# The first expert query ahead of the last input norm, its squares summed per token

## The reference

```
z = rmsnorm(h, norm2_g)                 # h / sqrt(mean(h*h) + EPS) * norm2_g
q = z @ peer_wq                         # 8 heads, two halves of 128 each
s1, s2 = q_half1 . keys1, q_half2 . keys2        # 128 + 128 scores per head
top 16 of each, their 256 sums, top 16 of these -> expert numbers, gate = softmax
act = gelu(u[expert] . z);  w = gate * act;  out = sum over experts of w * v[expert]
result = rmsnorm(h + out, norm_f_g)
```

## Time and profile before

| | |
|---|---|
| median of 3 runs | 2670.79 us (2670.49 to 2677.07) |
| span of the profiled execution, first to last instruction | 2671.2 us (the only time given for it) |
| busy PE, DVE, ACT, POOL | 2250.8, 2099.3, 1146.8, 639.4 us |
| traffic | 732.02 MB, 274 GB/s over the span |
| chain that ended last | DVE 23%, PE 17%, DMA 13%, issue 3% |

### The profile page before, as it was taken

One profiled execution on the slowest core, in us unless ns is written; L12 is line 12 of the kernel. 1 busy time (PEld: TensorE's weight loads), 2 busy tenths in 40 slices (PEclk: granted clock), 3 DMA queues, 4 the chain that ended last, 5 costly groups with the idle time before them and its releaser, 6 DMA issues.

```text
span 2671.2 us, 32182 instructions
## 1 busy us (share of the span) xinstructions
PE 2250.8 (84%) x11476; PEld 1809.5 (68%) x11476; DVE 2099.3 (79%) x2971; ACT 1146.8 (43%) x1721; POOL 639.4 (24%) x834
## 2 busy tenths in 40 slices
PE   8999989999999999989999964444555558999997
PEld 7997778888888888879888841111222225777776
DVE  6986647665566556578766999989999999999997
ACT  5433554443444344453542110000355444548876
POOL 1000000000000000000001353542444442786663
PEclk9999999999999999999999976555677778999999
DMA  6534344555555555545558999999999995899996
GB/s 226 179 129 110 111 157 158 188 189 188 189 188 188 185 186 183 168 128 173 165 167 343 422 420 419 420 419 420 419 417 409 420 418 208 347 405 409 409 409 271
DMA packets 314517, 732.02 MB, mean 274 GB/s; under 512 B 21040, under 2 KB 223024, under 8 KB 275760
## 3 DMA queue, kind: packets, MB, share of 16 engines
q0 software_dynamic: 73728, 402.69, 37.1%
q1 hardware_dynamic: 240544, 327.03, 35.9%
q10 hardware_dynamic: 144, 1.05, 0.1%
HBM read 728.61 MB, written 2.10 MB: 274 GB/s over the span
## 4 chain that ended last, share of the span: by engine, by line
DVE 23%; PE 17%; DMA 13%; issue 3%; POOL 2%; ACT 1%; DVEq 0%; SPq 0%; ACTq 0%; PEldq 0%; POOLq 0%
DVE row L2497 12%; DMA row<-in_peer_u,expert 8%; DMA row<-in_peer_v_rows,expert 5%; PE pg L1294 4%; PE pl L865 4%; PE pl L872 3%; DVE pl L2513 2%; POOL row L801 1%; PE pl L868 1%; PE pl L869 1%; DMA v_tile<-in_peer_v_dense 1%; PE pg L1285 1%; PE pl L1259 1%; PE pl L1188 1%; POOL spread_lo L776 1%
## 5 line engine op out<-in xcount | busy, mean ns | idle before, releaser
L1957 DVE TENSOR_TENSOR wlo<-raw,whi 128x1024 fp32r<-128x1024 f32 (+1 forms) x436 | 517.9, 1208 | 374.9 <-ACT whi L1341 373.3
L1341 ACT ACTIVATE whi<-raw 128x1024 fp32r<-128x1024 f32 (+1 forms) x436 | 444.6, 1039 | 412.0 <-PE pl L872 407.2
L2497 DVE CUSTOM_DVE_ANT_0 row<-row,pg 128x2048 f32<-128x2048 f32 x256 | 574.7, 2284 | 34.0 <-DMA row<-in_peer_u,expert 32.3
L1259 PE MATMUL pl<-row,diag 128*128 128x512 f32 x404 | 316.7, 930 | 333.6 <-DMA row<-in_peer_v_rows,expert 297.8
L865 PE MATMUL pl<-x_split,whi 128*128 128x512 f32 x1888 | 478.5, 395 | 10.2 <-DVE x_split L1965 5.3
L1259 PEld LDWEIGHTS pl<-row,diag 128*128 128x128 f32 x404 | 101.1, 276 | 500.2 <-issue 445.2
L865 PEld LDWEIGHTS pl<-x_split,whi 128*128 128x128 f32 x1888 | 341.5, 190 | 74.6 <-issue 7.5
L872 PE MATMUL pl<-x_split,wlo 128*128 128x256 f32 x2656 | 373.7, 284 | 3.9 <-DVE wlo L1957 3.9
L872 PEld LDWEIGHTS pl<-x_split,wlo 128*128 128x128 f32 x2656 | 359.0, 192 | 23.1 <-DVE wlo L1957 4.5
L801 POOL DMA_INDIRECT row<-in_peer_u,expert x256 | 242.8, 949 | 367.1 <-DVE dots L2497 155.7
L801 POOL DMA_INDIRECT row<-in_peer_v_rows,expert x256 | 261.4, 1021 | 199.4 <-DVE dots L2497 67.0
(11 more groups left out here) (348 smaller groups left out, 3041.6 us busy)
## 6 DMA issues: line engine op xcount, KB each, us to landing
v_tile<-in_peer_v_dense SPq DMA_DIRECT2D x128, 512.0 KB
raw<-in_w_in SPq DMA_DIRECT2D x51, 1024.0 KB
raw<-in_w_gate SPq DMA_DIRECT2D x44, 1024.0 KB
raw<-in_w_up SPq DMA_DIRECT2D x44, 1024.0 KB
raw<-in_w_out SPq DMA_DIRECT2D x32, 1024.0 KB
raw<-in_w_down SPq DMA_DIRECT2D x32, 1024.0 KB
wq<-in_peer_wq SPq DMA_DIRECT2D x15, 1024.0 KB, 11.5
raw<-in_w_down SPq DMA_DIRECT2D x16, 768.0 KB
```

What stands on the lines that cost most here:

```text
L1259: last = mm(pl_all[:, c:c + width], diag[:, (at - 1) % 4, :], row[b][:, c - DENSE:c - DENSE + width], start=at == 1, stop=at == ADDED_ROWS ...
L1341: return nc.scalar.activation(o, i, ACT.Copy)
L1957: V.tensor_tensor(wlo[:, n % 4, 0:k, :], w[:, :, f, :], whi[:, n % 4, 0:k, :].bitcast(F32), ALU.subtract)\
L2497: V.tensor_tensor_reduce(row[b][:], row[b][:], z_tok[:], 1.0, 0.0, ALU.mult, ALU.add, dots[:, at:at + 1])\
```

## The change

It does four things. The total of the squares is no longer made between the two halves of the first query, but behind the first scores, by `token_totals`: the squares are the stationary operand and a column of ones the moving one, so that a matmul leaves one total per token in one column of bank pl[3], tokens on partitions. DVE's `token_norm` makes mean and reciprocal of this 128x2 tile, placed between `experts(0, 8)` and the second half of the choice. ACT takes the root right into `small[:, 56:58]`, before the copy of transpose group 4; `rstd` is neither made nor turned. Group 4, which writes the bank of the totals, waits for DVE's reciprocal (`norm_inv`). And SP's weight loads 7 and 8 wait for all pieces but two, the loads from 9 on for all; the homes of tiles 8 and 9 are swapped for that.

```diff
--- before.py
+++ after.py
@@ -358,7 +358,7 @@
         scrap = sb("scrap", "raw", 0, [P, TT, D])
         diag = sb("diag", "rest", sq_sum_at, [P, 4, P])
 
-        wq_homes = [("tmp", D), ("arena", 2 * D), ("arena", 4 * D), *ring, ("whi", 0), ("whi", D), ("wlo", 0)]
+        wq_homes = [("tmp", D), ("arena", 2 * D), ("arena", 4 * D), *ring, ("whi", 0), ("wlo", 0), ("whi", D)]
         wq_homes += [("xlo", 0), ("xlo", D), ("wlo", D), *ring[1:]]
         wq = [sb(f"wq{m}", region, start, [P, KU, 2, P]) for m, (region, start) in enumerate(wq_homes)]
         qh = sq_r
@@ -389,6 +389,7 @@
 
         z_tok = pg_all
         pnorm = pg[3][:, 0:S]
+        ptotal = pl[3][:, 0:TT]
 
 
         x_in = [sem(f"x_in{c}") for c in range(4)]
@@ -449,7 +450,6 @@
         gelu_ready = sem("gelu_ready")
         z_scaled = sem("z_scaled")
         zgain_in = sem("zgain_in")
-        rstd_T = sem("rstd_T")
         rstd_tok = sem("rstd_tok")
         out1_ready = sem("out1_ready")
         out1_copied = sem("out1_copied")
@@ -675,7 +675,9 @@
                     slot_free(W0 + m - 3)
                 elif m == 7:
 
-                    sp.wait_ge(piece_used, PIECE0["out2"] + 32)
+                    sp.wait_ge(piece_used, PIECES - 2)
+                elif m == 9:
+                    sp.wait_ge(piece_used, PIECES)
                 elif m >= 13:
 
                     sp.wait_ge(wq_used, 3)
@@ -1209,12 +1211,11 @@
 
             def token_rows(t):
 
-                pe.wait_ge(norm_inv, NI["n2"] + 1)
                 for m in range(4 * t, 4 * t + 4):
                     f4 = m % 4
                     if m == 4:
 
-                        pe.wait_ge(rstd_tok, 1)
+                        pe.wait_ge(norm_inv, NI["n2"] + 1)
                     elif m == 5:
 
                         pe.wait_ge(sc_ready, 1)
@@ -1227,15 +1228,23 @@
                                                    res[:, f4 * 4 + f, t * P:(t + 1) * P], ident[:])
                     last.then_inc(tok_T, 1)
 
+            def token_totals():
+
+
+                pe.wait_ge(sq_added, 6 * (ADDED.index("n2") + 1))
+                pe.wait_ge(norm_sq, sq_count(NI["n2"], 7))
+                squares = (sq_sum[:, 0], sq_sum[:, 1], sq_r[:, 1, 0], sq_r[:, 1, 1])
+                for t in range(TT):
+                    for m, sq in enumerate(squares):
+                        last = mm(ptotal[:, t:t + 1], sq[:, t * P:(t + 1) * P], ones[:, 0:1], start=(m == 0), stop=(m == 3),
+                                  skip_group_check=True)
+                last.then_inc(norm_sum, 1)
+
             queries(0, (0,), (0,), q0_done)
             pe.wait_ge(z_scaled, 8)
-            wide_total("n2")
             queries(0, (1,), (0,), q0_done)
             peer_scores(0, (0,))
-
-            for t in range(TT):
-                last = nc.tensor.transpose(pl[3][:, t * P:(t + 1) * P], rstd[:, t * P:(t + 1) * P], ident[:])
-            last.then_inc(rstd_T, 1)
+            token_totals()
             token_rows(0)
             token_rows(1)
             queries(0, tokens=(1,))
@@ -1732,9 +1741,6 @@
                 query_squares(0, i)
             query_squares(7)
 
-            norm_root(NI["n2"])
-
-
             def late_query_weights(m):
 
                 nc.scalar.dma_start(wq[m][:].rearrange("p k f c -> p (k f c)"), A["peer_wq_2"][m]).then_inc(wq_in[m], 16)
@@ -1780,12 +1786,14 @@
                 act.wait_ge(fin_inv, t + 1)
                 activation(small[:, 36 + t:37 + t], small[:, 34 + t:35 + t], ACT.Sqrt).then_inc(fin_rstd, 1)
 
+            act.wait_ge(sq_added, 6 * (ADDED.index("n2") + 1))
             query_copy(0, (0,), q0_done, q0_ready)
             score_copy(0, (0,))
 
-            act.wait_ge(rstd_T, 1)
-            copy(small[:, 56:56 + TT], pl[3][:, 0:TT * P].rearrange("p (t c) -> p t c", t=TT)[:, :, 0]).then_inc(rstd_tok, 1)
             for m in range(8):
+                if m == 4:
+                    act.wait_ge(norm_inv, NI["n2"] + 1)
+                    activation(small[:, 56:56 + TT], small[:, 58:58 + TT], ACT.Sqrt).then_inc(rstd_tok, 1)
                 act.wait_ge(tok_T, m + 1)
                 t, f4 = m // 4, m % 4
                 copy(acc[:, t, f4 * 512:(f4 + 1) * 512], pg[f4] if t == 0 else pl[3 - m % 2]).then_inc(tok_r, 1)
@@ -2434,7 +2442,12 @@
                 weights_lo(u + 2, pc + 4, i=i, step=8)
                 out2_out(0, i)
             out2_out(7)
-            norm_scale(NI["n2"], D)
+
+            def token_norm():
+
+                dve.wait_ge(norm_sum, NI["n2"] + 1)
+                link(V.tensor_scalar(small[:, 58:58 + TT], ptotal, 1.0 / D, EPS, ALU.mult, ALU.add))
+                V.reciprocal(small[:, 58:58 + TT], small[:, 58:58 + TT]).then_inc(norm_inv, 1)
 
 
             def wide(ap, axis, shape):
@@ -2604,6 +2617,7 @@
             V.max_index(cpos[:, 0:8], ctop[:, 0:8], cand[:])
             link(V.match_replace(cand2[:], ctop[:, 0:8], cand[:], NEG))
             experts(0, 8, [work[:, m, :].rearrange("p (k j) -> p k j", k=8) for m in range(2)], sel_first)
+            token_norm()
             link(V.max(ctop[:, 8:16], cand2[:]))
             link(V.max_index(cpos[:, 8:16], ctop[:, 8:16], cand2[:]))
             V.tensor_tensor(gate[:, 0:TOPK], ctop[:], ctop[:, 0:1].broadcast_to([P, TOPK]), ALU.subtract).then_inc(sel_max, 1)
```

## The result

The changed kernel took 2677.26 us (median of 7 runs, 2674.93 to 2683.51) against 2670.98 (7 runs, 2670.27 to 2677.07) of the kernel before beside it: a ratio of 1.0022 [1.0011, 1.0032], 5.9 us slower (2.9 to 8.5; the differences in us here and below are the ratio's). The profiled execution has a span of 2675.4 us, before 2671.2. The forecast was 2675.5, a loss of 4.7 us: small, and within the 0.3% that was called "same".

The account below looks back on a forecast made before the run. From 1460 us on, DMA bytes were taken to set the time. Moved traffic 0, experts -1.72 (unused) and third row +4.7 on the profiled 2671.2 gave 2675.9, on the median's scale 2675.5 us; range 2669.0 to 2680.0.

Parts of the forecast that it names:

- The experts' 1.72 us, unused: Norm matmuls leave the first query, so MAX8 and the first eight experts come 1.72 us earlier, without use.
- The first gather: It waits for the last token copy, held behind norm_inv, and goes out at 1455.82, 1.83 us later.
- The third gather: It waits for the first query's weight buffer and moves from 1458.03 to 1462.32, before the clock's 2.0 us.
- The third row: Product of the third gather's row: 2.73 us later, 4.7 with the clock's 2.0; 5.89 us from issue to product.
- Behind it the queue is full, so this is the whole delay: After the third row the DMA queue is full, so that row's lateness is the whole stream's delay.
- The ninth gather: It waits for the second query, goes out at 1478.64, and lands in time by 0.7 us.
- The clock: PE's 4.4 us pause lowers TensorE's clock for 6.8 us: query loses 1.3, transposes 0.7, together 2.0 us.
- The loads, nothing: Weight loads 7 and 8 fill the DMA hole at 1430, but idle time moves before the first gather: 0 gained.
- No fall of the clock: Rival: PE's few matmuls in the pause, or where it falls, keep the clock up; +1.8 to +2.7, 2673.5; chance 0.20.
- A slow clock through the second query: Rival: the clock stays low until the second query is done; +17.5, 2688.3 us; chance 0.08.
- A gather with the experts: Rival: the last token copy ends by 1452.0, so all moves by -1.72, to 2669.1 us; chance 0.12.
- a filled hole that counts: Rival: loads and gathers overlap, so moving two 2.5 us loads gives -5.0, 2665.8 us; chance 0.06.

Follow-up runs that it names:

- PE kept busy: The changed kernel with 17 unread 128x128 matmuls in PE's pause before the fifth transpose group; ratio 1.0026 to the kernel before, in both tries.
- the query ahead: The changed kernel with the first query's other token half moved ahead of the second half of the token transposes; ratio 1.0017 to the kernel before.

## Why the prediction was right, and where its terms were off

*The experts' 1.72 us, unused*: right. MAX8 came 1.73 us earlier, and the kernel with another bank shows that even a gather that uses them changes nothing that can be measured while the third stays.

*The first gather*: the mechanism was right, the size low. Forecast with its 0.7 of the clock: +20.58; measured +21.70. The reciprocal ended at +16.31 and PE went on at +16.36 (forecast +16.43). Two terms failed. "From there the old spacings hold", 3.17 us to the end of the last copy, with 0.7 for the clock: it took 1452.91 - 1448.50 = 4.41, since the lower clock covered all the groups; with PE kept busy it took 3.13, so the spacings were right and the clock's share is 1.3. And POOL issued 0.93 us behind the end of the last copy, where I had put the 0.28 that it took behind the expert row.

*The third gather*: forecast 1462.32 - 1435.94 + 2.0 = +28.38, measured +28.47. The two errors cancelled: the query began at +19.92 (forecast +19.50), and its 128 records took 22.09 us against 21.13, 0.96 lost in place of 1.3. That this place came out to 0.1 us is luck.

*The third row*: forecast 4.7 later, measured 4.5 (+34.04 against +29.54); from issue to product 5.57 us, where 5.89 was taken. The fit of the Trainium skill (DMA: Bandwidth & Descriptors, "Anatomy of one DMA — SWDGE (gpsimd) path") gave an estimated 4.4 us and with it a sum of 3.8; the traces keep to the longer row.

*"Behind it the queue is full, so this is the whole delay"*: this step failed, by 0.6 to 0.9 us. The fourth row came 3.69 us behind the third (1469.87 - 1466.18), in place of 2.48 before, and the share in 1460 to 1464 was 0.81: one gather more does not yet fill the stream. By bytes the delay is 4.9 to 5.4 in the three traces with this pattern, where their third rows are late by 4.3 to 4.5; forecast 4.7. The third row came out a little early and the stream behind it lost a little more, so the 4.7 is nearer to the 5.4 than its parts deserve.

*The ninth gather*, "in time by 0.7 us": it went out at +42.79 (forecast +42.70), and the DMA share from +36 to +44 was 1.00. The margin held. Its own product came 7.3 us late, 9.8 us behind its issue (before 8.9); with the share at 1.00 I read this as other rows being moved meanwhile, which no run tests.

*The clock*: it fell, for 6.8 us as forecast, but 3.1 us after PE had stopped (1444.18) where the earlier pause had shown 5.1. It therefore took more from the transposes (1.2 in place of 0.7) and less from the query (1.0 in place of 1.3); the sum of 2.0 came out at 2.2. That it falls at a set distance from PE's stop was the weak premise: with the norm ahead of the experts it fell although PE had stood for only 0.80 and 0.96 us.

*The loads, nothing*: right, by two runs: moving them shifts the stream by 0.2 to 0.5 us and the time by nothing that can be told.

*The rivals.* No fall of the clock: it fell, and the kernel with PE kept busy shows what that rival would have been in the stream, 3.1, a little over its 1.8 to 2.7. A slow clock through the second query: it was back at 1454.1, under the first. A gather with the experts and a filled hole that counts: both refuted, the first by its releaser, the second by the loads alone.

*From the stream to the end.* A stream late by 5.4 and a time longer by 5.9 agree. Over all runs the stream's delay lies inside the interval of the time but for the changed kernel with the loads as before (4.9, just under its 5.3) and both tries with PE kept busy (3.1 and 3.2, under 4.3 and 4.5); what these lose beyond their stream was not found, and the changed kernel's second measurement (5.1 and 8.3) leans the same way. Spans can't refine it: the dense part, from the first to the last low tile, took between 375.0 and 379.4 us in the thirteen traces with no order in it (the kernel before 375.0, the changed one 377.8 and 379.1, the harmless other-bank kernel 379.4).

## What to carry to other kernels

A step that leaves the critical path can come back through a buffer: follow not only who reads its result, but who writes the bank it lies in. What a chain ahead of a full DMA stream costs is best read as bytes missing in a window with a fixed start in the program, which tells half a microsecond apart where the times of this kernel tell 3. And of several releases the one that comes last for a full queue counts: with the totals in another bank an earlier first gather brought nothing, since the third stayed, and with the query ahead an earlier third gather brought nothing, since the first came later. A run that takes a wait away should be read for what takes its place, here a table load and a fall of the clock.

## What was not expected of the hardware

- POOL issued its first gather 0.93 us behind the end of ACT's last copy in every trace in which that copy came last (the changed kernel, loads as before, PE kept busy, the norm early or late, the query ahead), and 0.28 or 0.29 behind DVE's expert row in the others. The runs don't tell whether the signal's engine or the order of POOL's two waits makes the difference.
- The clock fell 3.1 us after PE had stopped here and 5.1 after it in the earlier pause. Counted from the first query's start it fell at +15.1 to +15.3 in all five traces that show a fall, though PE stood for 4.3 us in three of them (two of the changed kernel and the loads as before), for 7.7 with the norm behind all experts, and for only 0.80 and 0.96 with the norm ahead. It stayed low for 6.8 us in the three, for 10.2 and for 3.4.
- The granted clock's 2 us, plain in the gathers' times and in the bytes, are not told by the kernel's time when the pause is filled.
- One and the same program reached its first query at 1432.1 and 1434.9 us in two executions (the changed kernel), at 1435.7 and 1432.3 (with PE kept busy). That is half of the whole effect and more, and over the thirteen traces the same point moves by 5.5 us; so a mark in the program is needed as zero.
